# Down projections of a two-layer decoder trunk: tiles 0 to 15 of the sum as block products eight tiles deep, six plain tiles ahead of them, two weight sums by transfers, another end of the run

## The reference

```python
def swiglu(h, w_gate_up, w_down):          # D_FF = 2816 = 22 * 128, D_MODEL = 1024
    gu = h @ w_gate_up
    g, u = gu[..., :D_FF], gu[..., D_FF:]
    return (jax.nn.silu(g) * u) @ w_down
...
    for layer in range(DEPTH):             # DEPTH = 2
        ...
        h = h + swiglu(rmsnorm(h, ffn_norm[layer]), ffn_w_gate_up[layer], ffn_w_down[layer])
    return rmsnorm(h, final_norm)
```

## Time and profile before

| | us |
|---|---|
| median of three runs (1385.14 to 1385.16) | 1385.14 |
| span of the profiled execution | 1383.4 |
| its down projection of layer 0 on PE | 509.77 to 626.34 |
| its down projection of layer 1 on PE | 1254.07 to 1375.20 |
| after the last matmul of that | 1375.20 to 1383.4 |

### The profile page before, as it was taken

One profiled execution on the slowest core, in us unless ns is written; L12 is line 12 of the kernel. 1 busy time (PEld: TensorE's weight loads), 2 busy tenths in 40 slices (PEclk: granted clock), 3 DMA queues, 4 the chain that ended last, 5 costly groups with the idle time before them and its releaser, 6 DMA issues.

```text
span 1383.4 us, 21582 instructions
## 1 busy us (share of the span) xinstructions
PE 1374.1 (99%) x8404; PEld 1225.5 (89%) x8404; DVE 961.5 (70%) x1335; ACT 663.8 (48%) x984; POOL 114.9 (8%) x89
## 2 busy tenths in 40 slices
PE   9999999999999999999999999999999999999997
PEld 8988888889999998998887788988888999998897
DVE  6656556469878877774578755765549888888674
ACT  6633534355455553352756634543454545545341
POOL 0012200110000000110211211100020000000011
PEclk9999999999999999999999999999999999999999
DMA  9721320222323233325321212542132223233321
GB/s 345 268 91 61 107 92 31 91 92 77 122 92 122 93 107 107 120 95 167 97 87 46 82 41 77 185 150 77 46 107 79 105 98 116 93 122 98 116 92 62
DMA packets 42285, 147.22 MB, mean 106 GB/s; under 512 B 5072, under 2 KB 5584, under 8 KB 42192
## 3 DMA queue, kind: packets, MB, share of 16 engines
q1 hardware_dynamic: 38592, 136.79, 28.8%
q10 hardware_dynamic: 3600, 9.12, 1.9%
HBM read 143.80 MB, written 2.10 MB: 105 GB/s over the span
## 4 chain that ended last, share of the span: by engine, by line
PE 96%; DVE 2%; issue 1%; ACT 1%; DMA 0%; POOLq 0%; POOL 0%; ACTq 0%; DVEq 0%
PE acc L2173 17%; PE acc L2175 17%; PE acc L2174 17%; PE acc L2521 8%; PE acc L2522 7%; PE acc L2523 7%; PE acc L2221 3%; PE acc L2223 3%; PE acc L2222 3%; PE aux L2572 2%; PE aux L2571 2%; PE aux L2570 2%; PE aux L2523 1%; PE aux L2522 1%; PE aux L2521 1%
## 5 line engine op out<-in xcount | busy, mean ns | idle before, releaser
L1304 DVE TENSOR_TENSOR w_lo<-raw,w_hi 128x1024 fp32r<-128x1024 f32 x165 | 205.6, 1251 | 123.6 <-ACT w_hi L663 123.2
L663 ACT ACTIVATE w_hi<-raw 128x1024 fp32r<-128x1024 f32 x165 | 173.2, 1052 | 98.6 <-PE acc L2175 55.2
L1229 POOL TENSOR_TENSOR sqsum<-sqsum,tmp 128x512 f32<-128x512 f32 x40 | 60.0, 1501 | 960.3 <-ACT tmp L950 637.0
L2173 PE MATMUL acc<-u_hi,w_hi 128*128 128x512 f32 x352 | 138.7, 394 | 0.0
L2175 PE MATMUL acc<-u_hi,w_lo 128*128 128x512 f32 x352 | 137.2, 390 | 0.0
L2174 PE MATMUL acc<-u_lo,w_hi 128*128 128x512 f32 x352 | 137.1, 389 | 0.0
L2521 PE MATMUL acc<-b_hi,s_hi 128*128 128x256 f32 x432 | 122.4, 283 | 0.0
L2522 PE MATMUL acc<-b_lo,w_hi 128*128 128x256 f32 x432 | 122.3, 283 | 0.0
L2522 PE MATMUL acc<-b_lo,s_hi 128*128 128x256 f32 x432 | 122.2, 283 | 0.0
L2523 PE MATMUL acc<-b_hi,w_lo 128*128 128x256 f32 x432 | 122.2, 283 | 0.0
L2523 PE MATMUL acc<-b_hi,s_lo 128*128 128x256 f32 x432 | 122.2, 283 | 0.0
(11 more groups left out here) (311 smaller groups left out, 3611.0 us busy)
## 6 DMA issues: line engine op xcount, KB each, us to landing
raw<-in_weights SPq DMA_DIRECT2D x253, 512.0 KB, 3.4
hT<-in_x_t ACTq DMA_DIRECT2D x4, 512.0 KB, 8.2
x_tok<-in_x ACTq DMA_DIRECT2D x4, 512.0 KB, 5.1
raw<-in_weights SPq DMA_DIRECT2D x5, 256.0 KB, 6.1
mem_tok<-in_mem ACTq DMA_DIRECT2D x2, 512.0 KB, 5.8
out_h<-out_f SPq DMA_DIRECT2D x2, 512.0 KB, 2.6
memT<-in_mem_t SPq DMA_DIRECT2D x3, 256.0 KB, 6.3
cs_d<-in_cs_d ACTq DMA_DIRECT2D x1, 512.0 KB, 4.3
```

Of the source, the lines that this page charges most:

```text
L663: act.activation(w_hi[:, s, :], raw[:, s, :], ACT.Copy).then_inc(hi_ready, 1)
L1229: pool.tensor_tensor(sqsum[:, :], sqsum[:, :], tmp[:, j % 2, :], ALU.add).then_inc(sq_added, 1)
L1304: dve.tensor_tensor(w_lo[:, s, :], raw[:, s, :], w_hi[:, s, :].bitcast(F32), ALU.subtract)\
L2173: pe.matmul(out, w_h, x_h, start=first, stop=False)
```

## The change

The down projection gets another division. Plain tiles now sum k = 16 to 21 alone (6 x 3 matmuls of 512 columns, one unit each), all eight of them first, with tiles 0 and 1 in two parts (k 16 to 19 of both, then k 20 and 21 of both). Then the four folds follow one after the other, eight tiles deep (k = 0 to 15, seven products of 8 x 3 matmuls of 256 columns, a whole ring of four units each). The activation operands are twice as large (128 x 2048) and all seven need buffers. Of the weight sums, POOL makes some by transfers: unit y gets unit x added by an adding transfer (`third_in`); `t_pre` is loaded from DRAM a second time and gets a unit added by another adding transfer (`pre_in`). DVE adds `t_mid` and `t_last` to them. `t_pre` and `t_mid` live in `memT`, so the odd layer loads `memT` again from ACT's queue. The orders of the queues of ACT, DVE and POOL are new. In the last layer the last tiles are now those of the last fold, with the first half's and second half's norm between its products. The host lays the units out accordingly.

```diff
-DOWN = (("p", 0), ("p", 1), ("p", 2), ("p", 3), ("f", 0), ("p", 4), ("f", 1), ("p", 5), ("f", 2), ("f", 3), ("p", 6), ("p", 7))
+LAST_ORDER = (1, 7, 6, 2, 4, 5, 3)
+FOLD_UNIT = {1: 0, 7: 1, 2: 2, 4: 3}
+PLAIN_K = 16
...
@@ ACT, ffn @@
+                def fold_hi_part(i, m):
+                    n = fold_unit(layer, i, m)
+                    act.wait_ge(raw_in[n % RING], 16 * (n // RING + 1))
+                    if m == 7:
+                        act.wait_ge(third_in, 16 * (fold_number(layer, i) + 1))
+                    slot_free(act, n - RING)
+                    act.activation(w_hi[:, n % RING, :], raw[:, n % RING, :], ACT.Copy).then_inc(hi_ready, 1)
+                def fold_sum_hi(i, m):
+                    if i:
+                        act.wait_ge(fold_done, fold_at(layer, i - 1, m))
+                    else:
+                        act.wait_ge(acc_done, a0 + A_DN + KT)
+                    if m == 5:
+                        act.wait_ge(pre_in, 32 * (fold_number(layer, i) + 1))
+                    else:
+                        act.wait_ge(lo_ready, fold_unit(layer, i, 7 if m == 6 else 4) + 1)
...
+                for j in range(KT - LEAD):
+                    split(u0 + F_DN + j + LEAD)
+                    for m in ((1,), (7, 2), (6,), (5,), (4, 3))[j]:
+                        fold_b_hi(m)
+                for m in (1, 7, 2):
+                    fold_hi_part(0, m)
+                fold_sum_hi(0, 6)
+                fold_hi_part(0, 4)
+                fold_sum_hi(0, 5)
+                fold_sum_hi(0, 3)
+                for i in range(FOLDS):
...
+                    fold_copy(i, 1)
+                    if not last:
+                        fold_hi_part(i + 1, 1)
...
+                    fold_copy(i, 7)
...
+                        fold_hi_part(i + 1, 7)
...
+                    fold_copy(i, 6)
+                    if not last:
+                        fold_hi_part(i + 1, 2)
+                        fold_sum_hi(i + 1, 6)
+                        fold_sum_hi(i + 1, 5)
+                        fold_hi_part(i + 1, 4)
+                        fold_sum_hi(i + 1, 3)
...
@@ POOL @@
+            def weight_sums(layer, i):
+                n = fold_number(layer, i)
+                x, y, z = [fold_unit(layer, i, m) for m in (1, 7, 4)]
+                pool.wait_ge(raw_in[y % RING], 16 * (y // RING + 1))
+                pool.dma_start(raw[:, y % RING, :], d["weights"][x], accum_op=ALU.add).then_inc(third_in, 16)
+                if n:
+                    pool.wait_ge(fslo_ready, fold_sums_at(layer, i, 5) - 3)
+                pool.dma_start(t_pre, d["weights"][y]).then_inc(pre_in, 16)
+                pool.wait_ge(pre_in, 32 * n + 16)
+                pool.dma_start(t_pre, d["weights"][z], accum_op=ALU.add).then_inc(pre_in, 16)
+            def down_sums(layer):
...
+                for i in range(FOLDS):
+                    weight_sums(layer, i)
+                    if i >= 2:
+                        add_squares(norm, 2 * i - 2, max(1, 2 * i - 4))
...
@@ DVE, ffn @@
+                def fold_mid(i):
+                    dve.wait_ge(pre_in, 32 * (fold_number(layer, i) + 1))
...
+                    dve.tensor_tensor(t_mid, t_pre, raw[:, fold_unit(layer, i, 1) % RING, :], ALU.add).then_inc(lo_ready, 2)
+                def fold_last(i):
...
+                    dve.tensor_tensor(t_last[:, :], t_mid, raw[:, fold_unit(layer, i, 2) % RING, :], ALU.add)                        .then_inc(lo_ready, 2)
...
                 up_second(PAIRS - 1)
                 split(u0 + F_DN + 2)
...
+                act_lo_part(10)
+                fold_b_sum(7)
+                split(u0 + F_DN + 3)
+                for m in (5, 6, 4):
+                    fold_b_sum(m)
+                down_tile(0)
+                split(u0 + F_DN + 4)
+                fold_b_lo(1)
+                down_tile(1)
+                split(u0 + F_DN + 5)
+                fold_b_lo(7)
+                down_tile(2)
+                split(u0 + F_DN + 6)
+                fold_b_lo(6)
+                down_tile(3)
+                split(u0 + F_DN + 7)
+                fold_b_lo(2)
+                down_tile(4)
+                fold_lo_part(0, 1)
+                down_tile(5)
+                fold_lo_part(0, 7)
+                fold_mid(0)
+                down_tile(6)
+                fold_lo_part(0, 2)
+                down_tile(7)
+                fold_sum_lo(0, 6)
+                fold_lo_part(0, 4)
+                fold_last(0)
+                fold_b_lo(5)
+                fold_sum_lo(0, 5)
+                fold_b_lo(4)
+                fold_sum_lo(0, 3)
+                fold_b_lo(3)
+                for i in range(FOLDS):
...
+                        fold_lo_part(i + 1, 1)
+                        fold_lo_part(i + 1, 7)
...
+                    fold_quarter(i, 11)
+                    fold_add(i, 11)
+                    if not last:
+                        fold_mid(i + 1)
+                        fold_lo_part(i + 1, 2)
...
+                    fold_quarter(i, 22)
+                    if not last:
+                        fold_sum_lo(i + 1, 6)
+                        fold_sum_lo(i + 1, 5)
...
+                    fold_quarter(i, 21)
+                    fold_add(i, 20)
+                    if not last:
+                        fold_lo_part(i + 1, 4)
...
+                    fold_add(i, 12)
+                    if not last:
+                        fold_last(i + 1)
+                        fold_sum_lo(i + 1, 3)
...
+                    fold_quarter(i, 22)
+                    fold_add(i, 22)
+                    last_scaled(0, range(3))
+                    fold_add(i, 12)
+                    last_scaled(0, range(3, 6))
                     last_var(1)
...
+                    last_scaled(0, range(6, KT))
+                    last_scaled(1, range(TURNED, KT))
...
@@ PE, ffn @@
+                for j in range(2):
+                    down_part(j, PLAIN_K, FT - 2)
+                for j in range(2):
+                    down_part(j, FT - 2, FT)
+                for j in range(2, KT):
+                    down_part(j, PLAIN_K, FT)
+                for i in range(FOLDS):
+                    if (layer, i) == (LAYERS - 1, FOLDS - 1):
                         break
...
+                    for m in FOLD_ORDER:
+                        fold(i, m)
```

More of the change, by code:

```diff
@@ L601, in program @@
                 used.append((None, product_at(layer, q, 4)))
-            for kind, j in DOWN:
-                if kind == "p":
-                    rows_used(F_ACC[layer] + A_DN + j, 1, 2)
-                else:
-                    used.append(("fold", fold_at(layer, j, 2)))
-                    used.append(("fold", fold_at(layer, j, 4)))
+            rows_used(F_ACC[layer] + A_DN, KT)
+            for i in range(FOLDS):
+                for m in FOLD_UNIT:
+                    used.append(("fold", fold_at(layer, i, m)))
         assert len(used) == UNITS
@@ L1001, in ffn @@
                     else:
[L1002 to L1004 removed]
+                        act_hi_part(9)
                         split(u0 + F_DN + 2)
@@ L1221, in norm_power, with add_squares @@
                 power(rstd_tok[:, :], var_e[:, :], TT)
-            def add_squares(norm, tiles=KT):
-                for j in range(1, tiles):
+            def add_squares(norm, tiles=KT, first=1):
+                for j in range(first, tiles):
                     n = (KT - 1) * (norm - 1) + j
@@ L1801, in fold_quarter @@
                     dve.wait_ge(fcopied, fold_copy_at(layer, i, of))
-                    part, copy = {11: (fold_c(layer, i), copy_1), 21: (fold_e(layer, i), copy_u),
-                                  22: (fold_a(layer, i), copy_7)}[c]
-                    dve.tensor_tensor(tmp[:, c // 20, half(1 if c == 22 else 0)], part, copy, ALU.add)\
+                    copy = {11: copy_1, 21: copy_u, 22: copy_7}[c]
+                    dve.tensor_tensor(tmp[:, c // 20, half(1 if c == 22 else 0)], fold_part(layer, i, m), copy, ALU.add)\
                         .then_inc(fquarter_ready, 1)
@@ L2862, in weight_units @@
         down = rows(w["ffn_w_down"][layer])
-        for kind, j in DOWN:
-            if kind == "p":
-                put(down[j:j + 1, :, UW:2 * UW])
-                put(down[j:j + 1, :, 2 * UW:DFF])
-            else:
-                put(down[2 * j:2 * j + 1, :, 0:UW])
-                put(np.concatenate([down[2 * j + 1, :, 512:1024], down[2 * j + 1, :, 0:512]], axis=1)[None])
+        put(down[:, :, 2 * UW:DFF])
+        for i in range(FOLDS):
+            top, bottom = down[2 * i], down[2 * i + 1]
+            for u in (top[:, 0:UW], bottom[:, 0:UW], top[:, UW:2 * UW], bottom[:, UW:2 * UW]):
+                put(u[None])
     assert n[0] == UNITS
```

524 lines of the change are left out of this document (224 added, 300 removed).

## The result

The changed kernel takes 1409.45 us (median, 1407.33 to 1413.17) against 1385.15: ratio 1.018, 95% interval 1.0166 to 1.0191. The forecast was 1389.4 with a range to 1398: the direction was right, the size was 20 us short. The profiled execution has a span of 1405.3 us and 2.0 us around it. Later comparisons ran the kernel before again; one of its executions took 7107 us and is left out of every number here.

What follows compares the result with a forecast made beforehand. PE, busy for 99% of the span, bounds the kernel. Layer 0 +2.3, layer 1 +1.3 and end +0.7 took 1383.4 to 1387.7; with 1.74 between span and median 1389.4 us, range 1383.5 to 1398.

Steps and rivals of the forecast that it cites:

- PE's own work: Matmuls per layer fall to 113.3 us (layer 1 keeps 3.5 more); 7.6 us saved in both layers if PE never waits.
- DVE's walk: DVE's queue in order: fold 0's quarter 22 done at 563.7; PE gaps 4.2 us per layer, at products 1, 6, 3.
- rival (a): POOL's transfers hide (P + A up to 8.5): 1385.8 to 1386.9 us, no change; chance 0.28.
- The transfers of POOL: Plain then adding transfer into t_pre take P + A = 9.2 us, adding 1.4 to the 4.2 us gap per layer.
- P: Time of POOL's plain transfer into t_pre, taken as 4.0 us, bounded by 3.2 and 5.4.
- A: Time of POOL's adding transfer into t_pre, taken as 5.2 us, bounded by 3.7 and 7.4.
- How the transfers reach PE: Late fold_mid(0) and fold_mid(1) hold quarter 22; past P + A = 8.5, each us costs about 2 per layer.
- Rival (b): Slow POOL transfers, P + A 11 to 12.8, gaps 9 to 13: 1396 to 1404; chance 0.22 with rival (c).
- rival (c): Gaps make PE's clock fall, each fall at most 2.9 us; with Rival (b) 1392 to 1402, joint chance 0.22.
- DVE and POOL's descriptors: DVE's instructions are all tensor_tensor, which does not lock GpSimd out while it writes descriptors; no cost to POOL's transfers.
- Later folds: Folds 1 to 3: quarter 22 done some 15 us in, product 3 at 17.3; cost nothing.
- The end: Tail after the last matmul: half of out_f0 leaves about 7 us later; +0.7 us, bounds 0 to 1.3.

Runs made afterwards that it cites:

- e13: e12 with POOL adding tile 2's square before waiting for fold 3's plain transfer, and ACT squaring tile 3 before sum 3's high part: 1383.57 us, ratio 0.9989.
- e14: e12 without POOL's three transfers per fold and the waits on them: 1380.57 us.
- e1: Changed kernel without POOL's three transfers per fold and the waits on them: 1387.57 us, ratio 1.0018.
- e6: Kernel before, plus a series of POOL transfers behind its last store, alone, in pairs, beside SP loads or DVE passes: plain 512 KB alone 3.7 and 3.5 us.
- e5: Changed kernel with 36, 12 and 14 dummy transposes ahead of fold 0's products 1, 6 and 3 to hold the clock up: 1409.16 us.
- after: The changed kernel itself, against the kernel before: 1409.45 us, ratio 1.018.
- e4: e2 plus reordered ACT and DVE queues (such as quarter 22 of fold 0 earlier): 1393.72 us.
- e8: e4 with fold 0's product 1 on its own semaphore, product 2's low part in DVE's pause, quarter 22 and sum 3 moved in all folds: 1386.75 us.
- e9: e8 with ACT's copy of product 6 moved ahead of the next fold's high part of unit 7: 1386.07 us, ratio 1.0009.
- e12: e9 with products 1 and 7 of all folds on their own counter and quarter 22 ahead of the next fold's first low parts: 1386.56 us.
- e2: Changed kernel with fold 0's two transfers into t_pre issued first in POOL's queue, ahead of the wait for unit y: 1399.51 us.
- e10: Changed kernel plus a second transfer series behind its last store, POOL's beside one, two and three SP loads: plain 4.3, 5.6, 7.0 us.

## Why the prediction was wrong, point by point

- **PE's own work: right.** 113.28 us were forecast; e13's layer 0 has 113.30, e14's too. In layer 1 both come within 0.1 us of the 116.8 forecast once their gaps and e14's low clock (1.7) are taken off. The 7.6 us of work are real, but no run has the whole of them in its time.
- **DVE's walk: right.** 4.2 us per layer in three named places; e1 has 3.9 in these places, and its 1387.57 stands where the sum without the transfers' share would be (1386.6; rival (a) ended at 1386.9).
- **The transfers of POOL: the step that failed, by its term P.** P = 4.0 and A = 5.2 are the lone prices, and e6 measured 3.6 and 5.3. In place the plain transfer took 8.2 us in fold 0 and 5.7 in fold 1, the adding one 5.1 and 5.3: A was right, P was far over its bound of 5.4. That bound was the longest landing of a load of SP's before, and it held a sign that was not read: before, a load issued alone took 3.2 us, and those issued 0.5 to 0.6 us behind another took 4.0 to 5.4. After, POOL issues an adding transfer 0.8 us ahead of the plain one, and SP loads the slots that the plain tiles free. Company was the missing term: 5.8 behind an adding one alone, 5.6 beside two loads, 7.0 beside three. That DMA had two thirds free as a mean was named for rival (a) and says nothing about these few us, in which it was 0.93 busy: these transfers are each waited for, so it is their length that counts.
- **How the transfers reach PE: right.** By the walk, pauses of 4.85 and 3.14 at the two t_mid put quarter 22 at 563.7 + 0.6 + 8.0 = 572.3; it ended at 572.4 (571.99 and 0.42). Rival (b), 1396 to 1404 with gaps of 9 to 13, had the mechanism, and the gaps of 10.55 and 10.8 lie in it; its chance of 0.22 was too low, and the result is 5 us beyond its end.
- **The clock (rival (c)): it fell, and half of it counted.** Two stretches per layer, 3.25 us in layer 0; the first lies inside the wait for product 3, the second costs 1.5 and 1.3 (e5 against after). Filling three of the four gave no gain in the median (e5). The range given for (c) together with (b), 1392 to 1402, lies below (b)'s own, though a fall can only add.
- **DVE and POOL's descriptors.** That all of DVE's instructions are tensor_tensor is not quite so: in layer 0 of after the passes at 519.0 and 521.3, and some from 632.7 on, are scalar_tensor_tensor. POOL's transfers run from 533.2 to 610.8, so nothing hangs on it.
- **Later folds: right for after, for a reason that was not seen.** They had no gap in after (but for the 0.8 in the last fold of layer 1), most likely since fold 0's gaps had given DVE time. In e4, e8, e9 and e12 gaps came up in them as those of fold 0 went. POOL's squares behind the landing (e12) were passed over: the text priced them only as contention with DVE.
- **The end: +0.7 forecast,** +0.4 measured in the tail.

With the measured pauses in place of the 1.4 us per layer, the prediction's own sum becomes 1385.1 - 7.6 + 2 x 12.2 + 0.4 = 1402.3. About 7 us remain. 1.6 are in layer 0 (13.8 over PE's work against 12.2), nearly all of it the second low stretch. 2.5 are in layer 1 (14.7 against 12.2): 1.4 of low clock, 0.8 at the last fold's product 3, and 0.3 of longer waits in fold 0. Another 0.6 is at the start of the run and 0.3 around the span, and by 2.1 the profiled execution, the shortest of four, lies under the median.

## What to carry to other kernels

Price a transfer that someone waits for by its length in the company that it will have there, not by its lone length or the mean load of the DMA engines, and count the issuer's own transfer just ahead as company. Look at what stands behind such a wait in every queue it touches. Here the gains came from order alone: issuing fold 0's two into t_pre 200 us earlier gave 9.9 us (e2), the order of ACT's and DVE's queues on top of it 5.8 (e4), a semaphore of its own for product 1 with quarter 22 and sum 3 moved in all folds 7.0 (e8), and squares moved past a wait 3.0 (e13). One copy moved ahead (e9), and products 1 and 7 on their own counter with quarter 22 earlier (e12), gave nothing that could be measured. And when a gap is mended, ask what the engine behind it did in that time: by these traces DVE's slack in fold 1 was fold 0's gap.

## What the runs showed of the hardware that was not expected

- POOL's plain transfer of 512 KB: 3.5 us alone, 4.3, 5.6, 7.0 beside one, two, three loads of the same size; the adding one 5.3, 7.5, 8.0, 9.4. Behind an adding one of POOL's, with no load, the plain one took 5.8. From ACT's queue, issued ahead of two loads, it took 4.6 (e6, e10, single transfers).
- Adding costs 1.7 us more than plain alone (5.3 to 3.6), 0.7 at 256 KB (3.7 to 3.0) and 0.5 at 128 KB (3.1 to 2.6).
- What a stretch of low clock costs depends on what PE waits for next. In layer 1 product 3 of fold 0 starts 62.4 us into the stage with a low stretch ahead of it (after) and 62.5 without one (e5); the stretch behind it, with no wait to hide in, cost 1.5 and 1.3 us.
- The length of a gap alone doesn't say whether the clock falls: behind e4's 2.9 us in fold 1 it fell to 0.50 in layer 1 and stayed full in layer 0, behind e9's 2.35 us it fell in layer 0 and not in layer 1.
